# Reordering the first mixing block of a two-block float32 layer, with shared preparation on GpSimd and an earlier overflow list

## What is computed

```python
mod = silu(c) @ w_ada + b_ada            # six rows of 1024
h = modulate(rms_norm(x, norm_mix), shift1, scale1)
g_q, g_k, g_v, g_z, g_a, g_b, s_q, s_k, s_v = split(h @ w_in)
gdn_out = gated_deltanet(g_q, g_k, g_v, g_z, g_a, g_b, ...)
swa_out = sliding_window_attention(s_q, s_k, s_v, q_norm, k_norm, sinks, positions)
x = x + gate1 * (concat([gdn_out, swa_out]) @ w_out)
h2 = modulate(rms_norm(x, norm_ffn), shift2, scale2)
x = x + gate2 * hierarchical_moe(h2, ...)   # 32 experts, two per token
```

## Time and profile before

| what | value |
|---|---|
| median of 3 runs | 2826.25 us (2822.76 to 2828.98) |
| the profiled execution | 2825.9 us |
| its span, first to last instruction | 2824.1 us |
| mean granted TensorE clock | 0.923 of 2.4 GHz |
| busy: PE | 2444.0 us (87%) |
| busy: DVE | 880.0 us (31%) |
| busy: ACT | 613.0 us (22%) |
| busy: POOL | 563.8 us (20%) |
| HBM read | 270.79 MB, 97 GB/s over the span |

### The profile page before, as it was taken

The page is one execution under the profiler, slowest core; times in us unless marked ns, Lnnn a source line. Parts: engine busy times, 40 slices in busy tenths (PEclk is TensorE's granted clock), DMA queues, the critical chain, the costliest instruction groups (busy, mean ns, idle before and its releaser), DMA issues.

```text
span 2824.1 us, 30509 instructions
## 1 busy us (share of the span) xinstructions
PE 2444.0 (87%) x12317; PEld 1887.2 (67%) x12318; DVE 880.0 (31%) x1282; ACT 613.0 (22%) x945; POOL 563.8 (20%) x182
## 2 busy tenths in 40 slices
PE   7994857986765999998799997799999977699997
PEld 5453436884533999994588785688875853588785
DVE  4314235432242011012422202333452941423302
ACT  1102322331101000011222212233333311222211
POOL 0000002220010000000434431433431410344331
PEclk8997978998778999999899998899999989899999
DMA  8220410000201788870122222222332222123221
GB/s 261 75 71 19 161 48 1 1 1 0 92 0 45 257 301 289 298 235 3 57 92 89 90 90 82 76 75 83 116 109 82 90 73 69 45 89 97 96 90 67
DMA packets 219925, 276.41 MB, mean 98 GB/s; under 512 B 9655, under 2 KB 199059, under 8 KB 219828
## 3 DMA queue, kind: packets, MB, share of 16 engines
q1 hardware_dynamic: 211744, 267.49, 28.8%
q0 software_dynamic: 1376, 4.26, 0.5%
q10 hardware_dynamic: 6708, 3.29, 0.4%
HBM read 270.79 MB, written 4.24 MB: 97 GB/s over the span
## 4 chain that ended last, share of the span: by engine, by line
PE 81%; DVE 9%; DVEq 3%; ACT 3%; issue 2%; DMA 1%; ACTq 1%; POOL 0%; SPq 0%; POOLq 0%
PE bank L2084 38%; PE bank L1761 8%; PE bank L1769 4%; PE bank L592 3%; PE bank L431 2%; PE bank L1559 2%; PE bank L575 2%; PE bank L2850 2%; PE bank L1971 2%; PE bank L1453 2%; PE bank L1243 1%; PE bank L2732 1%; PE bank L1236 1%; DVE arena L2819 1%; PE bank L2751 1%
## 5 line engine op out<-in xcount | busy, mean ns | idle before, releaser
L2084 PE MATMUL bank<-hT_high_split,ring_split 128*128 128x512 f32 x2496 | 797.2, 399 | 64.1 <-DVEq L2160 45.8
L2084 PEld LDWEIGHTS bank<-hT_high_split,ring_split 128*128 128x128 f32 x2496 | 472.1, 189 | 174.1 <-DVEq L2160 46.3
L2068 POOL TENSOR_TENSOR ring_split<-ring,ring_split 128x2048 fp32r<-128x2048 f32 x66 | 306.3, 4643 | 1080.5 <-ACT ring_split L2063 1080.5
L2084 PE MATMUL bank<-hT_split,ring_split 128*128 128x512 f32 x1248 | 491.9, 394 | 0.0
L2063 ACT ACTIVATE ring_split<-ring 128x2048 fp32r<-128x2048 f32 x104 | 198.9, 1915 | 700.5 <-DMA ring<-in_ffn_w_up 227.1
L2084 PEld LDWEIGHTS bank<-hT_split,ring_split 128*128 128x128 f32 x1248 | 236.4, 189 | 57.4 <-issue 0.2
L2308 POOL TENSOR_TENSOR ring_split<-ring,ring_split 128x2048 fp32r<-128x2048 f32 x38 | 176.2, 4639 | 373.0 <-ACT ring_split L2063 373.0
L1761 PE MATMUL bank<-arena,ring 128*128 x2048 | 235.3, 276 | 5.2 <-issue 5.2
L1761 PEld LDWEIGHTS bank<-arena,ring 128*128 128x128 f32 x2048 | 232.6, 193 | 5.4 <-issue 5.4
L2084 PE MATMUL bank<-ring_split,hid_high_split 128*128 128x512 f32 x704 | 225.4, 402 | 7.4 <-DVE hid_low_split L2170 7.4
L2084 PEld LDWEIGHTS bank<-ring_split,hid_high_split 128*128 128x128 f32 x704 | 134.5, 191 | 41.1 <-DVE hid_low_split L2170 8.2
(11 more groups left out here) (410 smaller groups left out, 2806.4 us busy)
## 6 DMA issues: line engine op xcount, KB each, us to landing
ring<-in_w_in SPq DMA_DIRECT2D x45, 1024.0 KB, 5.2
ring<-in_w_gate SPq DMA_DIRECT2D x32, 1024.0 KB, 5.5
ring<-in_w_up SPq DMA_DIRECT2D x32, 1024.0 KB, 8.0
ring<-in_w_down SPq DMA_DIRECT2D x32, 1024.0 KB, 7.5
ring<-in_ffn_w_gate SPq DMA_DIRECT2D x22, 1024.0 KB, 5.3
ring<-in_ffn_w_up SPq DMA_DIRECT2D x22, 1024.0 KB, 5.3
ring<-in_ffn_w_down SPq DMA_DIRECT2D x22, 1024.0 KB, 4.9
ring<-in_w_ada SPq DMA_DIRECT2D x16, 1024.0 KB, 5.2
```

Source lines behind the costliest of these rows:

```text
L2068: pool.tensor_tensor(low(n), raw(n), high(n).bitcast(F32), ALU.subtract)\
L2084: mm = pe.matmul(dst, left[l], right[r], start=start and n == 0, stop=stop and n == 2)
```

## The change

The projections of the attention come first, then qkv, then z. With them the preparation of the attention moves between the convolutions: DVE makes sums, angles, gate and rotation there, POOL the two rounds of multiplies. The preparation of the delta rule moves to the stretch before and during the z GEMM; three of its seven scalings stay with DVE, four go to POOL with the memsets. A barrier is gone, PE waits for `z_taken` before it transposes the queries. The second modulation row is turned in pieces inside the 16 units, out of a short row. Regions in SBUF move so that nothing overlaps that is now alive together. `dve_more_list` is called between the scatter rows and the copies of the gather, SP waits for the end of the gather only before the last of the three loads, and PE reports hT free earlier. The positions are loaded before the ring slots.

```diff
+plan("sq", n_slots(w_in, 2064, 2064 + 512))
+plan("skv", t_slots(w_in, 2576, 2832))
 plan("qkv", t_slots(w_in, 0, QKV))
 plan("z", n_slots(w_in, QKV, QKV + 512))
-plan("sq", n_slots(w_in, 2064, 2064 + 512))
-plan("skv", t_slots(w_in, 2576, 2832))
...
-    if u >= 1:
-        nxt(pe, "ada_taken")
+    pe_ada2_turn(pe, u - 1)
...
-    act.activation(ada_row[0:1, 256 * u:256 * u + 256], bank[7][0:1, 0:256], ACT.Copy)\
...
+    act.activation(ada_row[0:1, :], bank[7][0:1, 0:256], ACT.Copy).then_inc(S("ada_taken"), 1)
+
+def pe_ada2_turn(pe, u):
+    if u >= 0:
+        nxt(pe, "ada_taken")
+        for j in range(2):
+            mm = pe.matmul(bank[7][:, 256 + 2 * u + j:257 + 2 * u + j], ada_row[0:1, P * j:P * j + P],
+                           one[0:1, :], start=True, stop=True)
+        if u == 15:
+            mm.then_inc(S("ada_turned"), 1)
...
-    dve_mod(dve, 16, 48, 7)
+    dve_mod(dve, 16, 48, bank[7][:, 256:288])
...
 def pe_proj1(pe):
+    pe_gemm_n(pe, FIRST["sq"], tokens, bank[2:6])
+    nxt(pe, "wab_loaded", 16)
+    for t in range(NT):
+        for k in range(KD):
+            mm = pe.matmul(bank[6][:, 16 * t:16 * t + 16], tokens(k, t), wab[:, k, :],
+                           start=(k == 0), stop=(k == KD - 1))
+    mm.then_inc(S("ab_ps"), 1)
+    nxt(pe, "sq_taken")
+    need(pe, FIRST["skv"])
+    w = slot_view(FIRST["skv"], 256)
+    for t in range(NT):
+        for k in range(KD):
+            mm = pe.matmul(bank[2 + t][:, 0:256], tokens(k, t), w[:, k, :],
+                           start=(k == 0), stop=(k == KD - 1))
+    mm.then_inc(S("slots_used"), 1)
...
+    pe_gdn_sums(pe)
     nxt(pe, "conv_in", 2)
+
+def pe_z(pe):
+    nxt(pe, "skv_taken")
     pe_gemm_n(pe, FIRST["z"], tokens, bank[2:6])
...
-    nxt(pe, "z_taken")
...
 def act_proj1(act):
+    act.activation(g_ea, row("a_log").unsqueeze(1).broadcast_to([P, NT, H]), ACT.Exp)
+    nxt(act, "proj1_done")
+    act.activation(g_beta, b_in, ACT.Sigmoid).then_inc(S("g_beta"), 1)
+    nxt(act, "skv_taken")
+    act.activation(squares_q, sq, ACT.Square)
+    act.activation(squares_k, sk3, ACT.Square).then_inc(S("w_squares"), 1)
...
+        if m == 2:
+            nxt(act, "w_ss")
+            act.activation(w_r, w_ss, ACT.Sqrt, bias=eps, scale=1.0 / HD).then_inc(S("w_roots"), 1)
+        if m == 3:
+            nxt(act, "angles")
+            act.activation(sin, ang, ACT.Sin)
+            act.activation(cos, turns, ACT.Sin).then_inc(S("rotation"), 1)
+        if m == 4:
+            nxt(act, "g_abs")
+            act.activation(g_e, g_s, ACT.Exp, scale=-1.0).then_inc(S("g_exp"), 1)
...
+    dve.wait_ge(S("slots_used"), FIRST["sq"] + 2)
+    for t in range(NT):
+        i = dve.tensor_copy(sq[:, t, :], bank[2 + t][:, :])
+    i.then_inc(S("sq_taken"), 1)
+    nxt(dve, "ab_ps")
+    dve.tensor_copy(ab, bank[6][:, 0:64].rearrange("p (t n) -> p t n", n=16)).then_inc(S("proj1_done"), 1)
+    dve_angles(dve)
+    dve.wait_ge(S("slots_used"), FIRST["skv"] + 1)
+    for t in range(NT):
+        i = dve.tensor_copy(skv[:, t, :], bank[2 + t][:, 0:256])
+    i.then_inc(S("skv_taken"), 1)
...
+        dve_conv1(dve, m)
+        if m == 0:
+            dve_swa_sums(dve)
+        if m == 1:
+            dve_gdn_abs(dve)
+        if m == 2:
+            nxt(dve, "w_roots")
+            dve.reciprocal(w_ss, w_r).then_inc(S("w_recip"), 1)
+        if m == 5:
+            dve_gdn_gate(dve)
+        if m == 6:
+            nxt(dve, "w_normed")
+            nxt(dve, "rotation")
+        if 6 <= m < 6 + NT:
+            dve_rope(dve, m - 6)
+    dve.drain().then_inc(S("w_qk"), 1)
+
+def dve_z(dve):
     dve.wait_ge(S("slots_used"), FIRST["z"] + 2)
     for t in range(NT):
         i = dve.tensor_copy(z[:, t, :], bank[2 + t][:, :])
     i.then_inc(S("z_taken"), 1)
...
+ada_row = sm(800, 256)
+squares_q = region(16384, 2048, "p (t n) -> p t n", t=NT)
+squares_k = region(18432, 512, "p (t n) -> p t n", t=NT)
+kk = region(25680, 1024, "p (t g i e) -> p t g i e", t=NT, g=2, i=2)
...
-    nxt(dve, "w_roots")
-    dve.reciprocal(w_ss, w_r)
...
+def pool_swa_prep(pool):
+
+    nxt(pool, "w_recip")
+    for t in range(NT):
         k4 = sk3[:, t, :].rearrange("p (h e) -> p h e", e=HD)
-        dve.tensor_tensor(k4, k4, w_ss[:, t, H:NW].unsqueeze(2).broadcast_to([P, 2, HD]), ALU.mult)
-    dve.drain()
-    for t in range(NT):
-        dve.tensor_tensor(sq4[:, t], sq4[:, t], row("q_norm").unsqueeze(1).broadcast_to([P, H, HD]), ALU.mult)
+        pool.tensor_tensor(sq4[:, t], sq4[:, t], w_ss[:, t, 0:H].unsqueeze(2).broadcast_to([P, H, HD]), ALU.mult)
+        pool.tensor_tensor(k4, k4, w_ss[:, t, H:NW].unsqueeze(2).broadcast_to([P, 2, HD]), ALU.mult)
+    nxt(pool, "rows_loaded", 16 * len(ROWS))
+    pool.drain()
+    for t in range(NT):
         k4 = sk3[:, t, :].rearrange("p (h e) -> p h e", e=HD)
-        dve.tensor_tensor(k4, k4, row("k_norm").unsqueeze(1).broadcast_to([P, 2, HD]), ALU.mult)
-    nxt(dve, "rotation")
-    dve.drain()
+        pool.tensor_tensor(sq4[:, t], sq4[:, t], row("q_norm").unsqueeze(1).broadcast_to([P, H, HD]), ALU.mult)
+        i = pool.tensor_tensor(k4, k4, row("k_norm").unsqueeze(1).broadcast_to([P, 2, HD]), ALU.mult)
+    i.then_inc(S("w_normed"), 1)
...
+def dve_rope(dve, t):
     half = HD // 2
-    for t in range(NT):
-        for heads, src in ((H, sq4[:, t]), (2, sk3[:, t, :].rearrange("p (h e) -> p h e", e=HD))):
...
+        base = 16384 + 1024 * (t % 2) + (0 if heads == H else 2048)
+        u = [region(base + 256 * i, heads * half, "p (h f) -> p h f", f=half) for i in range(4)]
...
     nxt(pe, "w_qk")
+    nxt(pe, "z_taken")
...
-def dve_gdn_prep(dve):
+def dve_gdn_abs(dve):
...
     dve.scalar_tensor_tensor(g_s, g_u, -1.0, g_u, ALU.mult, ALU.max).then_inc(S("g_abs"), 1)
+
+def dve_gdn_gate(dve):
     nxt(dve, "g_exp")
...
+def dve_gdn_prep(dve):
+    nxt(dve, "g_sums")
...
     nxt(dve, "g_roots")
...
+    scaled(dve, kn, kn, g_ss[:, :, H:2 * H]).then_inc(S("g_normed"), 1)
+    scaled(dve, qn, qn, g_ss[:, :, 0:H])
+    dve.drain()
     nxt(dve, "g_exps")
...
+    scaled(dve, qg, qn, g_expG)
     dve.drain().then_inc(S("g_scaled"), 1)
...
+def pool_gdn_prep(pool):
+
+    nxt(pool, "g_beta")
+    nxt(pool, "qkv_taken", 3 * NT)
+    scaled(pool, vb, vb, g_beta)
+    nxt(pool, "g_normed")
+    nxt(pool, "g_exps")
+    scaled(pool, kdec, kn, g_kdec)
+    scaled(pool, kb, kn, g_beta)
+    pool.drain()
+    scaled(pool, kbG, kb, g_expG)
+    pool.memset(state, 0.0)
+    pool.memset(vnew, 0.0)
+    pool.drain().then_inc(S("g_parts"), 1)
...
     act.activation(squares, qkv[:, :, 0:1024], ACT.Square).then_inc(S("g_squares"), 1)
-    nxt(act, "g_abs")
...
-    act.activation(g_r, g_ss, ACT.Sqrt, bias=eps).then_inc(S("g_roots"), 1)
     nxt(act, "g_G")
     act.activation(g_expG, g_G, ACT.Exp)
     act.activation(g_kdec, g_kdec, ACT.Exp)
...
+    nxt(act, "g_ss")
+    act.activation(g_r, g_ss, ACT.Sqrt, bias=eps).then_inc(S("g_roots"), 1)
+
+def pe_gdn_sums(pe):
     nxt(pe, "g_ready")
...
-    nxt(pe, "g_scaled")
...
     nxt(pe, "h2_ready", NT)
+    pe.drain().then_inc(S("o_free"), 1)
...
+    dve_more_list(dve)
...
-    nxt(sp, "m_x_ps", 2 * KD)
+        sp.wait_ge(S("m_x_ps"), 2 * KD)
-    pe.drain().then_inc(S("o_free"), 1)
...
+    sp_positions(sp)
-    sp_positions(sp)
...
+    nxt(act, "rows_loaded", 16 * len(ROWS))
-    meet(act)
-    act_swa_prep(act)
+    act_gdn_prep(act)
-    act_gdn_prep(act)
...
-    meet(pe)
+    pe_z(pe)
-    pe_gdn_prep(pe)
+    nxt(pe, "g_scaled")
+    nxt(pe, "g_parts")
...
-    dve_mod(dve, 0, 16, 7)
+    dve_mod(dve, 0, 16, bank[7][:, 0:16])
+    nxt(dve, "rows_loaded", 16 * len(ROWS))
-    meet(dve)
-    dve_swa_prep(dve)
+    dve_gdn_prep(dve)
+    dve_z(dve)
-    dve_gdn_prep(dve)
...
-    dve_more_list(dve)
...
-    meet(pool)
+    pool_swa_prep(pool)
+    pool_gdn_prep(pool)
```

More of the change, by code:

```diff
@@ L197, in build @@
         rstd = sb("rstd", [P, NT])
-        ARENA = 29900
+        ARENA = 30096
         A = sb("arena", [P, ARENA])
@@ L411, in dve_ada1, with dve_mod @@
                 mm.then_inc(S("ada_sums"), 1)
-        def dve_mod(dve, m0, m1, b):
-            dve.tensor_tensor(mod[:, m0:m1], bank[b][:, m0:m1], cols1[:, m0:m1], ALU.add)
+        def dve_mod(dve, m0, m1, sums):
+            dve.tensor_tensor(mod[:, m0:m1], sums, cols1[:, m0:m1], ALU.add)
             dve.drain()
@@ L631, in act_proj1, with dve_conv1 @@
                 act.activation(convT[:, m, :], convacc[:, m % 2, :], ACT.Silu).then_inc(S("silu_done"), 1)
+        def dve_conv1(dve, m):
+            at, _ = col("conv_w", VEC1)
+            j = m % 2
+            nxt(dve, "conv_in")
+            if m >= 2:
+                nxt(dve, "silu_done")
+            dve.drain()
+            dve.tensor_scalar(convacc[:, j, :], convin[:, j, 3:3 + T], cols1[:, at + 36 + m:at + 37 + m],
+                              None, ALU.mult)
+            for tap in range(3):
+                dve.drain()
+                w = cols1[:, at + 12 * tap + m:at + 12 * tap + m + 1]
```

(30 more changed lines are left out.)

129 lines of the change are left out of this document (18 added, 111 removed).

## The result

The changed kernel takes **2741.19 us** (median of 4 runs, 2739.38 to 2743.36) against 2827.19 for the kernel before on the same chip (4 runs, 2822.76 to 2828.98): ratio 0.9698, 95% interval 0.9682 to 0.9715. The profiled execution took 2742.18, span 2740.3, mean granted clock 0.936 (before 0.923).

A forecast was written before the change was run, and what follows sets the result against it. TensorE carries four fifths of the chain of waits, so only its idle or low-clock stretches count. Terms -24.7 -3.4 -35.1 -3.9 -18.0 = -85.1 take 2825.9 to 2740.8, said as 2741 us; range 2730 to 2758.

The forecast's parts named there:

- E: Rival: tail and clock terms smaller than charged (no slow transposes, warm start of both loops), 2732; chance 0.08.
- Turn to the query transposes: First block up to attention: reordered GEMMs let query transposes start at 239.3 instead of 264.00, -24.7 us.
- The tail: Behind the qkv GEMM: PE waits 4.9 us for the last silu, then transposes take 8.0 plus 1.0.
- Attention, -3.4: Second modulation row's 64 one-column matmuls, turned inside 16 units, cost 7.3 us instead of 10.7; bounds 0 and -4.3.
- Delta-rule preparation, -35.1: Start of the delta rule: the hole from 398.07 to 433.34 goes, except 0.2 us for the barrier.
- Clock, -3.9: Matmuls behind the two removed holes, query transposes and delta-rule start, run faster; bounds -1 and -6 us.
- Overflow item, -18.0: After the gather: early list starts the item at 878 instead of 895.19, plus 0.8 for clock; bounds -15 and -20.
- PE's entry into the loop: Overflow item: after the gate matmuls PE pays a loop entry, hidden before, giving a start of 878.
- What I had costed at nothing: Work moved under other work, load order and added waits, and POOL and DVE overlapping: 0 us, far end +20.
- rival A: POOL slower or blocking DVE longer, delaying rotations, convolutions and z's copies: up to +20, 2761, middle 2752; chance 0.17.

The follow-up runs named there:

- units2: Changed kernel with TensorE's wide modulation matmuls before the weight turn in attention units 5, 9 and 13, and the last unit's behind its values: 2740.08 us.
- outs: Changed kernel with VectorE taking a token tile's outputs one attention unit later, behind the maxima of units 5, 9 and 13: 2717.41 us, ratio 0.9602 to before.
- pool_more: Changed kernel with 24 more GpSimd 128x512 multiplies ahead of the eight that normalise queries and keys, results unused: 2758.45 us, +17.3.
- units: Changed kernel with TensorE's wide modulation matmuls before the weight turn, not behind, in attention units 5, 9 and 13: 2740.0 us, ratio 0.9694.
- both: Kernel with TensorE's attention order changed, plus half of z before the qkv transposes and eight delta-rule query scalings inside attention units: 2741.66 us.

## Why the prediction was right, and where its terms were not

The forecast was -85.1; the profiled execution gave 2825.9 - 2742.2 = -83.7. The mechanism is the one forecast, and no rival took place (of E only the shorter tail). By its own steps:

- **Turn to the query transposes, -24.7: -27.4.** The tail was right: 5.1 us from the last qkv matmul to the transposes (4.9 forecast), 8.90 for the 48 transposes (9.0). Two charges were too high. The projections ended at 192.5 instead of 193.8, since the whole stage began 0.65 earlier, the ab matmuls took 8.16 instead of 10.62 and the qkv GEMM 82.41 instead of 84.05, though the first GEMM paid for its start (30.35 for 27.73) and the key/value one took 16.13 for 15.3. And z took 27.48, not 28.9: the granted clock was 0.94 in the last 6 us of the transposes and 1.00 in z. The copies took their 2.6.
- **Attention, -3.4: mis-sized.** A turn of one unit at the full clock is 0.53 us, 0.13 per matmul, not 0.10, and those behind stalls take 1.01. The stage was 2.7 us shorter, of which 1.5 are the warmer query transposes, which I had booked under the clock. The turns by themselves gave 0 where they were the only edit. The window of 20 in 2.00 us was the fastest stretch of the block, and I took it for the price.
- **Delta-rule preparation, -35.1: -34.7.** The undo measured +30.3, as the gate stays out of the hole; POOL's share did not shorten it.
- **Clock, -3.9: it was not there.** The transposes gave their -1.5. But the delta rule starts cold even though PE waits only 1.23 us: twelve matmuls in 2.98 (2.93 before), with a granted clock of 0.66 and then 0.50. I had tied the low clock to the 35 us hole, and it came without one. With the wide modulation matmuls last (`units2`) these twelve went at 1.00, which speaks for the narrow work at the end of the attention as a cause, though the wait ahead of them was also shorter there (0.65 for 1.23). In `outs`, with the narrow work and the wait of 1.23 as they were, the first eight took only 1.25 us, so neither is shown to be the whole cause. The stage was 2.5 longer, not 2.7 shorter.
- **Overflow item, -18.0: -20.5, and -20.0 alone.** The item's own stretch became 0.7 shorter besides, so that -21.2 stands against the forecast. It was too small by what I had charged for PE's entry into the loop. I had taken it from SP's 2.1 and PE's 5.23 at other places, and PE goes from the gate matmuls into the item with no idle time. The rows of DVE and SP of the changed kernel are: list ready at 760, first weights issued at 762.42, the last at 800.69, and it landed 4.9 us later, ahead of 810.17.

```profile
759.42 0.91 DVE L1936 MEMSET arena<- 128x1024 f32 x1 [0.32 <-issue]
...
762.42 0.39 SPq L1956 DMA_DIRECT2D hT<-in_w_gate  x1
...
800.69 0.38 SPq L1959 DMA_DIRECT2D arena<-in_w_down  x1
```

The way to the query transposes and the item brought 2.7 and 3.2 more than forecast, the clock (+1.0 for -3.9) and the turns of the modulation row 4.9 and 2.2 less. The 2.3 between output GEMM and gather had no term, and the 1.9 lost in the expert loop and behind it had none either. The total is closer than its parts, by luck.

What I had costed at nothing held, by its margins. POOL's prices for 128x512 were not 1.05 throughout. Single lines of the changed kernel (ns min/median/max, first and last start us):

```profile
L799 POOL TENSOR_TENSOR arena<-arena x4: 1038/1044/1509, 136.8 to 141.0; 128x512 f32<-128x512 f32 x4
L805 POOL TENSOR_TENSOR arena<-arena,rows x4: 1257/1626/1708, 143.5 to 149.8; 128x512 f32<-128x512 f32 x4
L1044 POOL TENSOR_TENSOR arena<-arena x16: 1043/1236/1488, 207.2 to 233.8; 128x512 f32<-128x512 f32 x16
L1044 DVE TENSOR_TENSOR arena<-arena x12: 684/1450/1530, 216.5 to 228.3; 128x512 f32<-128x512 f32 x12
```

Beside DVE they took up to 1.71, the attention's part ended at 151.9 instead of about 150, and the first rotation came at 164.05: 12 us of cover, where I had 13 (and 14 in the sum of rival A). DVE's part of the delta-rule preparation was ready at 229.8, between my 225.7 and 234.1, and 4.2 before z ended; POOL's, with the memsets, at 236.2, where I had said by 240. The Trainium skill (SBUF — State Buffer, section Who interferes with whom) has the two exclude each other for the whole instruction. The trace agrees in direction and not in full size: 8 POOL and 8 DVE multiplies, 1.04 and 0.61 each when alone, would be 13.2 us in turn and took 10.5. Rival A needed a POOL price far above these and with it the loss of the cover; `pool_more` shows that once the cover is gone the delay comes through.

The one place that I read and did not price was the stall in three units. It stood in my rows as an example of a low clock, and was worth 24 us for one line of code.

## What to carry to other kernels

A short stall on TensorE costs itself and the slow matmuls behind it: here 4.1 us idle cost 7 to 8 with them, so three short stalls inside a busy loop were worth more than the 4.3 us behind a GEMM. Before a stalled engine's own order is changed, follow the wait to the first engine that stands idle in front of work that is ready; changing the order at the end of the chain only renames the wait. Moving work to GpSimd pays where VectorE is idle or the bound lies elsewhere, not beside a VectorE burst on the same memory, and a cover should be checked against the price with both engines running.

## What the runs showed of the hardware that I had not expected

- Two-input fp32 multiplies of 128x512: DVE alone 0.61 us each, POOL alone 1.04; both at once 0.66 us per multiply over the two, no faster than DVE alone.
- The granted clock of the first delta-rule matmuls was 0.50 behind a wait of 1.2 us as behind one of 35. With the wide modulation matmuls last in attention it was 1.00 there, with no gain in total time. The delta-rule stage with the same code took 239.1, 243.0 and 246.0 us in three kernels, with a granted clock of 1.00, 0.73 and 0.50 in the 12.5 us behind its first 4, and again 246.0 when the changed kernel ran once more; what brings the clock back sooner or later stays open.
- The narrow ab matmuls (L589) took 8.16 us in the changed kernel and 8.30 when it ran once more, but 11.14 and 11.17 in `units` and `units2`, and 8.47 in `both`, which has their order of PE too; the source up to there is the same in all. Differences of 3 us at one place of one profile are no evidence, and the totals hardly show them.
